# The next head's gates scaled on ScalarE, and two clamps placed at two levels of the recurrence

## The chip, the cores and the metric

The kernel runs on one core of one Trainium2 chip. The metric is the device time of one execution in microseconds (us). The core has a matrix engine (PE in the profile, with its weight loads as PEld), VectorE (DVE), ScalarE (ACT), GpSimd (POOL), a queue that issues nearly all transfers (SP, SPq in the profile) and 16 DMA engines. Each engine works through its own list of instructions in order and waits on semaphores that others raise.

## The reference, cut to what matters

The model is one encoder block over 1280 tokens of width 1024 (a prompt of 256 and a sample of 1024): layer norm, one wide projection, neighbourhood attention, a gated linear recurrence in two directions, a mix of the two branches, and an expert-choice feed-forward layer with 16 experts. The change lies in the recurrence, which has 4 heads of 128 channels:

```python
def forget_gates(z, lb):
    f = lb + (1.0 - lb) * jax.nn.sigmoid(z)
    log_f = jnp.log(jnp.maximum(f, F_MIN))
    k = (1.0 - lb) * jax.nn.sigmoid(-z)
    return k, log_f
# hgrn2_chunk_scan, for each direction: b = cumsum(log_f) within a chunk;
#   a[t, s] = sum_k q[t, k] * k[s, k] * exp(b[t, k] - b[s, k])   for s <= t
#   o = (q * exp(b)) @ S + a @ v;   S carries k and v from chunk to chunk
```

`lb` is one lower bound for each direction and channel. The gates of one head are two arrays of 128 channels by 1280 tokens, one for each direction `d`.

## The kernel before, in words

The stages follow one another, each in a block with a barrier behind it: front (layer norm and projection), attention, recurrence (`stage_recurrence`), mixing, choice of tokens, experts. The recurrence runs from about 612 to 1007 us of the span.

A head of the recurrence is computed in `R = 9` rounds, numbered `r` from 0. Rounds 0 and 1 make the keys for the carried state and round `r >= 2` makes the weights of one of `LEVELS = 7` levels, by which the 128x128 matrix of a chunk is filled in halves. A level takes these steps, one on each engine:

- POOL (L1027 `difference`) and DVE (L1297 `differences`) subtract running sums and write a slot of `W`; there are `WS = 3` slots, and a slot comes free when the matrix engine has read the level three before (`wait_slot`, L939).
- ACT (L1184 `exp`) takes the exponential of the whole slot, 128x2560.
- DVE (L1303 `weights`) multiplies by queries and keys: one product of 128x1280 at L1307 and two of 128x640 at L1314, then raises `w_ready`.
- PE (L1083 `pairs`) waits for that and runs 20 products of 128x128 (L1098).
- DVE (L1318 `gather`) copies what is valid of the level (L1331).

The product of round `r` is `pairs(r - 1)`. Between these products PE runs filler (L1047 `fill`): the last part of the wide projection, 40 units of two halves, 12 matmuls of 128x512 each half (L1062 to L1064). One half stands ahead of `pairs(n)` and one behind it. A unit needs a tile of the input (`fx`, two buffers, loaded at L977), its weights (`fw`, a ring of 11 blocks, loaded at L969 when a slab of 10 units ends) and one of two accumulators, which ACT empties at L1155 (`evict`).

During head `hd` the gates of head `hd + 1` are prepared. ACT calls `gates` in round 3, after its exponential: for each direction two sigmoids (L1165 into `f`, L1166 in place of the input `k`), then Silu of the queries (L1168). DVE calls `prepare` at the end of its own round 3 (L1371): for each direction it scales `k` (L1278), scales and shifts `f` (L1280), writes `lf = max(f, LN_SPLIT)` (L1283) and clamps `f` to the range from F_MIN to LN_SPLIT (L1285). ACT takes the logarithms of both in round 5 (L1170 `logarithms`, waiting for `clamped`), and DVE sums them with scans after its last round (L1288 `run_sums`). A function of another table costs ACT a load of a table (ACT_TABLE_LOAD).

The order of every engine's list is written out by hand in the four `head` functions. The lines that the change touches are L1160 to L1168 for ACT and L1271 to L1286, L1371 and L1378 for DVE.

Of the kernel before, what the change touches and what calls it, by code (L numbers as in the profile page):

```python
# [22 lines left out]
F32 = mybir.dt.float32  # L23
# [4 lines left out]
ACT = mybir.ActivationFunctionType  # L28
ALU = mybir.AluOpType
AX = mybir.AxisListType  # L30

P = 128
# [4 lines left out]
NT = T // P  # L37
# [3 lines left out]
HG_HEADS = 4  # L41
# [15 lines left out]
F_MIN = 1e-30  # L57
# [770 lines left out]
LN_SPLIT = 2.0 ** -60  # L828


def stage_recurrence(nc, ident, h, hT, xs, ws, lb_fwd, lb_bwd, o, room, carry, fw, fx, fw_in, fx_in,
# [24 lines left out]
    MASKS = 1 + 2 * LEVELS  # L856
    SETUP, PER = 5 + 3 + MASKS, 3 * 2
    U = len(LATER) * NT
    with ExitStack() as ctx:
        s = Stage(nc, ctx, "hg")  # L860
        k = [carry[:, 0:2 * T].rearrange("p (d t) -> p d t", d=2), s.sb("k", [P, 2, T])[:]]
        qT = [carry[:, 2 * T:3 * T], s.sb("qT", [P, T])[:]]
        v = [carry[:, 3 * T:4 * T].rearrange("p (c t) -> p c t", c=NT), s.sb("v", [P, NT, P])[:]]
        f, lf = s.sb("f", [P, 2, T]), s.sb("lf", [P, 2, T])
        E = s.sb("E", [P, 2, NT, P + 1])
        W = s.sb("W", [P, WS, 2, T])
        qi = room[:, 0:2 * T].rearrange("p (d t) -> p d t", d=2)
        kiT = room[:, 2 * T:4 * T].rearrange("p (d c t) -> p d c t", d=2, c=NT)
        decay = s.sb("decay", [P, 2, NT])
        S = s.sb("S", [P, 2, NT, P])  # L870
        A = room[:, 4 * T:5 * T]
        mask = s.sb("mask", [P, LEVELS, 4 * P], U8)
# [3 lines left out]
        lb, omlb = s.sb("lb", [P, 2, HG_HEADS]), s.sb("omlb", [P, 2, HG_HEADS])  # L876
# [9 lines left out]
             "lb_in", "iota_done", "q_done", "z_done", "clamped", "ln_done", "scanned",  # L886
             "dec_done", "pool_d", "dve_d", "exp_done", "w_ready", "qi_done", "ki_turned", "ki_copied", "l_mm",
             "a_done", "ds_mm", "s_made", "o_mm", "o_copied", "stored", "chain", "lb_ready"))
        fx_half = s.sem("fx_half")
        f_copied, f_stored = s.sem("f_copied"), s.sems("f_stored", 2)  # L890
        ki_groups = [(0, a, n) for a, n in CHUNK_GROUPS] + [(1, a, n) for a, n in reversed(CHUNK_GROUPS)]

# [57 lines left out]
        with nc.Block() as block:  # L950
# [193 lines left out]
            def _(act):  # L1144
# [15 lines left out]
                def gates(p, w):  # L1160
                    act.wait_ge(k_in[w], 32 * (p // 2) + 32)
                    if p >= 1:
                        act.wait_ge(scanned, 2 * p)
                    for d in range(2):
                        nc.scalar.activation(f[:, d], k[w][:, d], ACT.Sigmoid)  # L1165
                        nc.scalar.activation(k[w][:, d], k[w][:, d], ACT.Sigmoid, scale=-1.0).then_inc(z_done, 1)  # L1166
                    act.wait_ge(q_in[w], 16 * (p // 2) + 16)
                    nc.scalar.activation(qT[w], qT[w], ACT.Silu).then_inc(q_done, 1)  # L1168

# [64 lines left out]
            def _(dve):  # L1234
# [33 lines left out]
                          .then_inc(chain, 1)  # L1268
                        dve.wait_ge(chain, step.next())

                def prepare(p, w):  # L1271

                    count_of = Steps(PER)
                    count_of.base = SETUP + p * PER if p else SETUP - MASKS
                    for d in range(2):
                        dve.wait_ge(z_done, p * 2 + d + 1)
                        one_less, low = (x[:, d, p:p + 1] for x in (omlb, lb))
                        nc.vector.tensor_scalar(k[w][:, d], k[w][:, d], one_less, None, ALU.mult).then_inc(chain, 1)  # L1278
                        count_of.next()
                        nc.vector.tensor_scalar(f[:, d], f[:, d], one_less, low, ALU.mult, ALU.add).then_inc(chain, 1)  # L1280
                        dve.wait_ge(chain, count_of.next())

                        nc.vector.tensor_scalar(lf[:, d], f[:, d], LN_SPLIT, None, ALU.max).then_inc(chain, 1)  # L1283
                        dve.wait_ge(chain, count_of.next())
                        nc.vector.tensor_scalar(f[:, d], f[:, d], F_MIN, LN_SPLIT, ALU.max, ALU.min)\  # L1285
                          .then_inc(clamped, 1)  # L1286

                def run_sums(p):  # L1288
                    for d in range(2):
# [6 lines left out]
                def head(hd, w):  # L1296
                    def differences(r):  # L1297
                        if r >= 2:
                            wait_slot(dve, hd, r)
                            to, a, b = exponents(r)[3]  # L1300
                            nc.vector.tensor_tensor(to, a, b, ALU.subtract).then_inc(dve_d, 1)

                    def weights(r):  # L1303
                        dve.wait_ge(exp_done, hd * R + r + 1)
                        z, y = W[:, r % WS, 0], W[:, r % WS, 1]
                        if r >= 2:
                            nc.vector.tensor_tensor(z, z, qT[w], ALU.mult)  # L1307
                        else:
                            nc.vector.tensor_tensor(y, y, k[w][:, r], ALU.mult).then_inc(w_ready, 1)
                            return  # L1310
                        m = P >> (r - 1)
                        for side in range(2):
                            part = halves(chunked(y), m, side)
                            last = nc.vector.tensor_tensor(part, part, halves(chunked(k[w][:, side]), m, side),  # L1314
                                                           ALU.mult)
                        last.then_inc(w_ready, 1)

                    def gather(n):  # L1318

                        for g, (a, count) in enumerate(CHUNK_GROUPS):  # L1320
                            cols, width = slice(a * P, (a + count) * P), count * P
                            dve.wait_ge(l_mm, (hd * NL + n) * NG + g + 1)
                            if n == 0:
                                if hd >= 1:
                                    dve.wait_ge(stored, 16 * hd)
                                nc.vector.tensor_tensor(chunked(A[:, cols]), chunked(l_ps[g][:, 0:width]),
                                                        ident[:].unsqueeze(1).to_broadcast([P, count, P]), ALU.mult)\
                                  .then_inc(a_done, 1)
                            else:
                                dve.wait_ge(a_done, (hd * NL + n - 1) * NG + g + 1)  # L1330
                                nc.vector.copy_predicated(A[:, cols], mask[:, n - 1, 0:width], l_ps[g][:, 0:width])\  # L1331
                                  .then_inc(a_done, 1)

                    def states():

                        dve.wait_ge(dec_done, hd + 1)
                        steps = 0
                        for n, (d, a, count) in enumerate(ki_groups):
                            dve.wait_ge(ds_mm, hd * 2 * NG + n + 1)
                            order = list(range(a, a + count))  # L1340
                            for c in order if d == 0 else reversed(order):
                                to = c + 1 - 2 * d
                                if c in (ends, starts)[d]:
                                    continue
                                steps += 1
                                add = ring[n % NR][:, (c - a) * P:(c - a + 1) * P]
                                if c in (starts, ends)[d]:
                                    nc.vector.tensor_copy(S[:, d, to, :], add).then_inc(s_made, 1)
                                else:
                                    nc.vector.scalar_tensor_tensor(S[:, d, to, :], S[:, d, c, :], decay[:, d, c:c + 1],  # L1350
                                                                   add, ALU.mult, ALU.add).then_inc(s_made, 1)
                                dve.wait_ge(s_made, hd * NS + steps)

                    weights(0)
                    weights(1)
                    differences(2)
                    dve.wait_ge(q_done, hd + 1)
                    if hd >= 1:
                        dve.wait_ge(o_mm, hd * NG)
                    for d in range(2):  # L1360
                        nc.vector.tensor_tensor(qi[:, d], W[:, d, 0], qT[w], ALU.mult).then_inc(qi_done, 1)
                    gather(0)
                    for r in range(2, R):
                        if r + 1 < R:
                            differences(r + 1)
                        weights(r)
                        if r == 2:
                            states()
                        if r >= 3:
                            gather(r - 2)  # L1370
                        if r == 3 and hd + 1 < HG_HEADS:  # L1371
                            prepare(hd + 1, 1 - w)
                    if hd + 1 < HG_HEADS:
                        dve.wait_ge(pool_d, (hd + 1) * R)
                        run_sums(hd + 1)
                    gather(R - 2)

                prepare(0, 0)  # L1378
                masks()
                run_sums(0)  # L1380
                for hd in range(HG_HEADS):
# [650 lines left out]
PER = 2  # L2032
# [761 lines left out]
def build(nc, x, ln_in_g, ln_in_b, w_in, rpb, lb_fwd, lb_bwd, norm_g, w_na, w_hg, w_out, ln1_g, ln1_b, w_router,  # L2794
# [9 lines left out]
    with ExitStack() as ctx:  # L2804
        s = Stage(nc, ctx, "main")
        ident = s.sb("ident", [P, P])
        stage_consts(nc, ident)
        routing, mix = ctx.enter_context(ExitStack()), ctx.enter_context(ExitStack())
        with ExitStack() as bias:
            b = Stage(nc, bias, "bias")  # L2810
# [83 lines left out]
```

## Time and profile before

| what | value |
|---|---|
| median of 3 runs (2830.43 to 2831.44) | 2831.01 us |
| span of the profiled execution, first to last instruction | 2824.7 us |
| busy: PE, DVE, ACT, POOL | 2684.5 (95%), 1835.0 (65%), 1396.6 (49%), 557.2 (20%) us |
| mean granted PE clock | 0.977 of full speed |
| tile load of the filler (page, DMA issues) | 1024.0 KB, 5.3 us to landing |

No time of its own is listed for the profiled execution beside its span. The 6.3 us between span and median lie outside the first and the last instruction. A busy PE is not PE at its peak: the filler's matmuls are recorded as 0.39 to 0.40 us each and start 0.23 us apart, so busy time counts overlap once and says only that there is no hole.

### The profile page before, as it was taken

How to read it: one execution, taken by the hardware profiler on the slowest of the kernel's cores; microseconds unless marked ns; L12 is line 12 of the kernel's file. 1: busy time of each engine (PE TensorE's matmuls, PEld its weight loads, DVE VectorE, ACT ScalarE, POOL GpSimd, SP SyncE). 2: the span in 40 equal slices, each digit the busy share in tenths (PEclk: the TensorE clock that was granted, in tenths of full speed). 3: DMA queues.
4: the chain of work that ended last, by engine and by line, in shares of the span. 5: the costliest groups of instructions: out<-in, count | busy, mean ns of one | idle time of the engine just before them, and what ended most of it. 6: DMA issues, size and time to landing. Idle time of an engine off the chain costs nothing.

```text
span 2824.7 us, 44574 instructions
## 1 busy us (share of the span) xinstructions
PE 2684.5 (95%) x18224; PEld 2149.7 (76%) x18224; DVE 1835.0 (65%) x2309; ACT 1396.6 (49%) x1769; POOL 557.2 (20%) x492
## 2 busy tenths in 40 slices
PE   7999999988999979994999999999999999999998
PEld 5788887877887858883677777777777777777776
DVE  6212231768889756657577667677667667667888
ACT  2211221865555443341556656556656656656765
POOL 2000030004443523431001001101011001101334
PEclk9999999999999989996999999999999999999999
DMA  6478875766565554435678878878877878878984
GB/s 231 161 194 236 254 258 138 164 226 222 197 224 183 182 193 138 145 109 214 222 281 284 310 276 305 294 274 296 315 273 286 310 275 304 308 274 322 372 317 152
DMA packets 237452, 686.26 MB, mean 243 GB/s; under 512 B 18729, under 2 KB 65208, under 8 KB 232128
## 3 DMA queue, kind: packets, MB, share of 16 engines
q1 hardware_dynamic: 219904, 627.96, 62.5%
q0 software_dynamic: 17344, 55.44, 7.2%
q8 instruction: 145, 2.38, 0.3%
q14 instruction: 59, 0.48, 0.1%
HBM read 577.46 MB, written 105.88 MB: 242 GB/s over the span
## 4 chain that ended last, share of the span: by engine, by line
PE 49%; POOL 1%; DMA 1%; issue 1%; ACT 0%; DVE 0%; POOLq 0%; ACTq 0%; DVEq 0%
PE moe_strip L2453 12%; PE moe_up L2468 4%; PE moe_down L2468 4%; PE moe_gate L2468 4%; PE moe_gate L2470 4%; PE moe_down L2469 4%; PE moe_gate L2469 4%; PE moe_down L2470 4%; PE moe_up L2469 4%; PE moe_up L2470 4%; PE moe_up L2394 1%; POOL moe_minus_mean L2280 0%; PE moe_turn L2428 0%; DMA y<-moe_out_p,moe_at_out 0%; PE moe_gate L2403 0%
## 5 line engine op out<-in xcount | busy, mean ns | idle before, releaser
L2661 DVE TENSOR_TENSOR pieces_low<-pieces_raw,moe_high 128x1024 fp32r<-128x1024 f32 x768 | 893.2, 1217 | 355.2 <-PE moe_strip L2453 344.6
L2553 ACT ACTIVATE moe_high<-pieces_raw 128x1024 fp32r<-128x1024 f32 x768 | 769.3, 1051 | 360.2 <-PE moe_up L2470 195.8
L2453 PE MATMUL moe_strip<-pieces_raw,moe_xT_p 128*32 128x256 f32 x4096 | 230.5, 383 | 1.0 <-ACT moe_xT_p L2565 1.0
L2453 PEld LDWEIGHTS moe_strip<-pieces_raw,moe_xT_p 128*32 128x32 f32 x4096 | 130.6, 111 | 96.8 <-issue 13.9
L2468 PE MATMUL moe_gate<-moe_high,moe_xT 128*128 128x512 f32 x512 | 202.3, 395 | 2.0 <-DVE pieces_low L2661 1.9
L1031 POOL TENSOR_TENSOR hg_W<-hg_E 128x640 f32<-128x640 f32 (+1 forms) x92 | 164.4, 1814 | 196.8 <-PE hg_l L1098 99.5
L2468 PE MATMUL moe_up<-moe_high,moe_xT 128*128 128x512 f32 x512 | 202.9, 396 | 0.0
L2468 PE MATMUL moe_down<-moe_high,moe_hdn 128*128 128x512 f32 x512 | 202.6, 396 | 0.2 <-DVE pieces_low L2661 0.2
L2470 PE MATMUL moe_gate<-pieces_low,moe_xT 128*128 128x512 f32 x512 | 199.7, 390 | 0.0
L2469 PE MATMUL moe_up<-moe_high,moe_xT 128*128 128x512 f32 x512 | 199.6, 390 | 0.0
L2469 PE MATMUL moe_down<-moe_high,moe_hdn 128*128 128x512 f32 x512 | 199.5, 390 | 0.0
L2469 PE MATMUL moe_gate<-moe_high,moe_xT 128*128 128x512 f32 x512 | 199.5, 390 | 0.0
L2470 PE MATMUL moe_down<-pieces_low,moe_hdn 128*128 128x512 f32 x512 | 199.4, 390 | 0.0
L2470 PE MATMUL moe_up<-pieces_low,moe_xT 128*128 128x512 f32 x512 | 199.1, 389 | 0.0
L2244 POOL COPY moe_at_in<-main_picks 32x1 uint32<-32x1 uint32 (+1 forms) x32 | 10.4, 352 | 784.3 <-PE moe_up L2394 775.7
L492 DVE COPY fr_out<-fr_acc 128x512 f32<-128x512 f32 (+1 forms) x28 | 17.8, 634 | 194.1 <-PE fr_acc L361 106.7
L1062 PE MATMUL hg_facc<-bias_fw,bias_fx 128*128 128x512 f32 x320 | 132.2, 413 | 11.8 <-PEq L103 5.4
L1064 PE MATMUL hg_facc<-bias_fw,bias_fx 128*128 128x512 f32 x320 | 127.1, 397 | 0.0
L1063 PE MATMUL hg_facc<-bias_fw,bias_fx 128*128 128x512 f32 x320 | 126.9, 396 | 0.0
L2468 PEld LDWEIGHTS moe_up<-moe_high,moe_xT 128*128 128x128 f32 x512 | 96.0, 188 | 32.3 <-issue 13.2
L2468 PEld LDWEIGHTS moe_down<-moe_high,moe_hdn 128*128 128x128 f32 x512 | 96.1, 188 | 26.2 <-issue 6.6
L2453 PE MATMUL moe_strip<-pieces_raw,moe_hdn_p 128*32 128x256 f32 x2048 | 113.8, 380 | 0.0
(363 smaller groups left out, 5655.6 us busy)
## 6 DMA issues: line engine op xcount, KB each, us to landing
pieces_raw<-in_w_gate_e SPq DMA_DIRECT2D x128, 1024.0 KB, 5.3
pieces_raw<-in_w_up_e SPq DMA_DIRECT2D x128, 1024.0 KB, 7.0
pieces_raw<-in_w_down_e SPq DMA_DIRECT2D x128, 1024.0 KB, 5.1
bias_fx<-xs SPq DMA_DIRECT2D x40, 1024.0 KB, 5.3
fr_raw<-in_w_in SPq DMA_DIRECT2D x16, 1024.0 KB, 7.9
ws<-fr_late_split SPq DMA_DIRECT2D x32, 512.0 KB, 4.7
bias_fw<-ws SPq DMA_DIRECT2D x32, 512.0 KB, 8.6
mo_gates<-h SPq DMA_DIRECT2D x20, 512.0 KB, 4.5
```

What stands on the lines that cost most here:

```text
L492: nc.vector.tensor_copy(out[:, n, 0:width(i)], src).then_inc(copied[n], 1)
L1031: last = nc.gpsimd.tensor_tensor(to, a, b, ALU.subtract)
L1062: nc.tensor.matmul(f_acc[i % 2][:], fx[:, i % 2, 0, c, :], hi, start=(c == 0), stop=False)
L1063: nc.tensor.matmul(f_acc[i % 2][:], fx[:, i % 2, 0, c, :], lo, start=False, stop=False)
L1064: last = nc.tensor.matmul(f_acc[i % 2][:], fx[:, i % 2, 1, c, :], hi, start=False, stop=(c == KD - 1))
L2394: last = nc.tensor.transpose(to[:, k * P:(k + 1) * P], rows_s[:, (4 * j + k) * P:(4 * j + k + 1) * P], ident[:])
L2453: last = nc.tensor.matmul(strip_ps[j * CP:(j + 1) * CP, kind, :], x, raw[g % RAW][:, k * D + j * STRIP:k * D + (j + 1) * STRIP], start=sta ...
L2468: nc.tensor.matmul(to[:], x_k[:, kk, 0:CS], hi, start=(kk == 0), stop=False)
L2469: nc.tensor.matmul(to[:], x_k[:, kk, CS:2 * CS], hi, start=False, stop=False)
L2470: return nc.tensor.matmul(to[:], x_k[:, kk, 0:CS], lo, start=False, stop=(kk == count - 1))
L2553: nc.scalar.activation(high[:, g % HI, cols], raw[g % RAW][:, cols], ACT.Copy).then_inc(hi_done, 1)
L2661: nc.vector.tensor_tensor(low[g % RAW][:, cols], raw[g % RAW][:, cols], high[:, g % HI, cols].bitcast(F32), ALU.subtract).then_inc(lo_done, 1)
```

## The change

ACT takes over the scaling of `k` and of `f` for heads 1 to 3, behind the four sigmoids of round 3 and ahead of Silu. DVE keeps the two clamps of each direction; direction 0 is clamped in round 3 and direction 1 in round 4. Head 0's gates, which are made before the first round, stay as they were (`prepare_first`). `decay` is allocated ahead of `W` instead of behind it, and an unused tensor of 32 bytes per partition is allocated on the right side of the memory for the whole program.

```diff
-        E = s.sb("E", [P, 2, NT, P + 1])
+        E, decay = s.sb("E", [P, 2, NT, P + 1]), s.sb("decay", [P, 2, NT])
         W = s.sb("W", [P, WS, 2, T])
...
-        decay = s.sb("decay", [P, 2, NT])
...
-        fx_half = s.sem("fx_half")
+        fx_half, z_opened = s.sem("fx_half"), s.sem("z_opened")
...
                     for d in range(2):
                         nc.scalar.activation(f[:, d], k[w][:, d], ACT.Sigmoid)
-                        nc.scalar.activation(k[w][:, d], k[w][:, d], ACT.Sigmoid, scale=-1.0).then_inc(z_done, 1)
+                        nc.scalar.activation(k[w][:, d], k[w][:, d], ACT.Sigmoid, scale=-1.0)\
+                          .then_inc(z_opened if p else z_done, 1)
+                    for d in range(2 if p else 0):
+                        one_less, least = (x[:, d, p:p + 1] for x in (omlb, lb))
+                        act.wait_ge(z_opened, (p - 1) * 2 + d + 1)
+                        nc.scalar.activation(f[:, d], f[:, d], ACT.Identity, bias=least, scale=one_less)
+                        nc.scalar.activation(k[w][:, d], k[w][:, d], ACT.Copy, scale=one_less).then_inc(z_done, 1)
...
-                def prepare(p, w):
+                def clamp(d, count):
+
+                    nc.vector.tensor_scalar(lf[:, d], f[:, d], LN_SPLIT, None, ALU.max).then_inc(chain, 1)
+                    dve.wait_ge(chain, count)
+                    nc.vector.tensor_scalar(f[:, d], f[:, d], F_MIN, LN_SPLIT, ALU.max, ALU.min).then_inc(clamped, 1)
+
+                def prepare_first():
...
+                def prepare(p, d):
+
+                    dve.wait_ge(z_done, p * 2 + d + 1)
+                    clamp(d, SETUP + PER + (p - 1) * 2 + d + 1)
...
-                        if r == 3 and hd + 1 < HG_HEADS:
-                            prepare(hd + 1, 1 - w)
+                        if r in (3, 4) and hd + 1 < HG_HEADS:
+                            prepare(hd + 1, r - 3)
...
-                prepare(0, 0)
+                prepare_first()
...
+        ctx.enter_context(nc.sbuf_tensor("side_pad", [P, 8], F32, side="right"))
```

`prepare_first` holds the eight instructions of the old `prepare` for head 0, the last two of each direction through `clamp`.

## Rows read from the trace of the kernel before

**Rows 1.** Windows: heads 0 and 3. Start:end, length, each engine's busy time (instructions), clock, DMA.
```profile
663.00:743.20 80.20, 75.32 (x446) 66.27 (x444) 68.28 (x96) 42.71 (x39) 32.92 (x20) 0.98 0.58 200
...
926.60:1000.60 74.00, 73.74 (x447) 65.17 (x446) 54.12 (x70) 23.62 (x22) 32.03 (x19) 1.00 0.52 173
```

**Rows 2.** Timeline of PE: start, duration, engine, line, operation, tiles, [idle before <- releaser].
```profile
685.05 2.39 PE L1098 MATMUL hg_l<-hg_W 128*128 128x128 f32 x20
687.20 0.48 PE L1062 MATMUL hg_facc<-bias_fw,bias_fx 128*128 128x512 f32 x1
...
692.78 2.39 PE L1098 MATMUL hg_l<-hg_W 128*128 128x128 f32 x20
...
705.36 3.93 PE L1098 MATMUL hg_l<-hg_W 128*128 128x128 f32 x20 [4.70 <-DVE bias_table L1331]
...
714.61 2.39 PE L1098 MATMUL hg_l<-hg_W 128*128 128x128 f32 x20
...
793.17 4.07 PE L1098 MATMUL hg_l<-hg_W 128*128 128x128 f32 x20 [4.70 <-DVE bias_table L1331]
```

**Rows 3.** Windows: the products behind the hole of head 0, columns as in rows 1.
```profile
705.30:709.20 3.90, 3.84 (x21) 3.87 (x22) 3.90 (x6) 3.89 (x5) 0.00 (x0) 0.60 1.01 422
```

**Rows 4.** Waits of PE's weight loads: total us, times, longest.
```profile
PEld hg_l L1098 <- DVE hg_W L1314: 15.3, 3, 5.1
```

**Rows 5.** Timeline of DVE in rounds 3 and 4 of head 0.
```profile
689.13 1.74 DVE L1278 TENSOR_SCALAR hg_k<-hg_k,hg_omlb 128x1280 f32<-128x1280 f32 x1
690.79 1.99 DVE L1280 TENSOR_SCALAR hg_f<-hg_f,hg_omlb,hg_lb 128x1280 f32<-128x1280 f32 x1
...
694.42 0.88 DVE L1278 TENSOR_SCALAR hg_k<-hg_k,hg_omlb 128x1280 f32<-128x1280 f32 x1
695.22 0.94 DVE L1280 TENSOR_SCALAR hg_f<-hg_f,hg_omlb,hg_lb 128x1280 f32<-128x1280 f32 x1
...
699.75 1.96 DVE L1301 TENSOR_TENSOR hg_W<-hg_E 128x640 f32<-128x640 f32 x1
...
703.03 1.55 DVE L1314 TENSOR_TENSOR hg_W<-hg_W,wroom 128x640 f32<-128x640 f32 x2
```

**Rows 6.** Source line L1283, all instances: shortest, median, longest ns.
```profile
L1283 DVE TENSOR_SCALAR hg_lf<-hg_f x8: 827/828/1806, 629.0 to 873.8; 128x1280 f32<-128x1280 f32 x8
```

**Rows 7.** Windows: two rounds of head 3, which prepares no gates, columns as in rows 1.
```profile
953.20:968.66 15.46, 15.46 (x90) 13.48 (x89) 11.54 (x14) 5.66 (x4) 9.59 (x6) 1.00 0.52 170
```

**Rows 8.** Timeline of DVE in head 1: a pair of products that ran beside POOL's.
```profile
805.77 3.67 DVE L1314 TENSOR_TENSOR hg_W<-hg_W,hg_k 128x640 f32<-128x640 f32 x2
```

**Rows 9.** Timeline of ACT: around the gates in head 0, and one eviction in head 1.
```profile
677.51 1.26 ACT L1166 ACTIVATE hg_k<-hg_k 128x1280 f32<-128x1280 f32 x1
...
681.25 0.58 ACT L1155 ACTIVATE bias_table<-hg_facc 128x512 f32<-128x512 f32 x1
685.25 0.60 ACT L1155 ACTIVATE hg_fout<-hg_facc 128x512 f32<-128x512 f32 x1 [3.41 <-PE hg_facc L1064]
...
687.16 2.35 ACT L1195 ACTIVATE hg_W<-hg_W 128x2560 f32<-128x2560 f32 x1
...
785.79 0.60 ACT L1155 ACTIVATE hg_fout<-hg_facc 128x512 f32<-128x512 f32 x1 [3.46 <-PE hg_facc L1064]
```

**Rows 10.** Groups by line and shape, ACT: count | busy us, mean ns | idle before.
```profile
L807 ACT ACTIVATE na_sc<-na_sc,na_nmax 128x512 f32<-128x512 f32 x32 | 23.0, 719 | 2.3 <-DVE na_nmax L765 1.5
...
L389 ACT ACTIVATE fr_late_split<-fr_late 128x512 fp32r<-128x512 f32 x32 | 20.2, 630 | 110.7 <-DMA fr_late<-in_w_in 110.5
```

**Rows 11.** Timeline of SP: the first loads of the filler's next weights in head 0.
```profile
697.97 3.04 SPq L969 DMA_DIRECT2D bias_fw<-ws  x5
```

**Rows 12.** Source line L969, all 21 loads: us from issue to landing.
```profile
DMA to landing us min/median/max: 3.2/6.2/10.2
```

**Rows 13.** Source line L1307, by tile: shortest, median, longest ns.
```profile
L1307 DVE TENSOR_TENSOR hg_W<-hg_W,wroom x14: 1476/1484/2573, 669.8 to 903.4; 128x1280 f32<-128x1280 f32 x14
L1307 DVE TENSOR_TENSOR hg_W<-hg_W,hg_qT x14: 1472/1492/2576, 757.8 to 988.2; 128x1280 f32<-128x1280 f32 x14
```

More of the change, by code:

```diff
@@ L1269, in masks @@
                         dve.wait_ge(chain, step.next())
-                def prepare(p, w):
+                def clamp(d, count):
[3 more added lines that the diff above has]
+                def prepare_first():
                     count_of = Steps(PER)
-                    count_of.base = SETUP + p * PER if p else SETUP - MASKS
+                    count_of.base = SETUP - MASKS
                     for d in range(2):
-                        dve.wait_ge(z_done, p * 2 + d + 1)
-                        one_less, low = (x[:, d, p:p + 1] for x in (omlb, lb))
-                        nc.vector.tensor_scalar(k[w][:, d], k[w][:, d], one_less, None, ALU.mult).then_inc(chain, 1)
+                        dve.wait_ge(z_done, d + 1)
+                        one_less, low = (x[:, d, 0:1] for x in (omlb, lb))
+                        nc.vector.tensor_scalar(k[0][:, d], k[0][:, d], one_less, None, ALU.mult).then_inc(chain, 1)
                         count_of.next()
@@ L1281, in prepare @@
                         dve.wait_ge(chain, count_of.next())
[L1283 to L1286, printed above, removed]
+                        clamp(d, count_of.next())
+                def prepare(p, d):
+                    dve.wait_ge(z_done, p * 2 + d + 1)
+                    clamp(d, SETUP + PER + (p - 1) * 2 + d + 1)
                 def run_sums(p):
```

## The prediction

> **What bounds the kernel now.** I read the page first. PE is busy 95% of the span, so in most stages the other engines don't matter; only a hole in PE is worth anything. The table of windows, taken head by head, finds where the holes are: head 0 of the recurrence takes 80.20 us from its first product to its last level, head 3 takes 74.00 us, and both run the same 447 or so matmuls. In head 3 PE has no hole to speak of (73.74 us busy) at a clock of 1.00; in head 0 it is busy 75.32 us at 0.98 [rows 1]. Head 3 is the only one that prepares no gates.
>
> The timeline of PE shows the difference at one place. Level products normally start 7.73 us apart (685.05, 692.78), with two halves of filler between them. The next one, `pairs(3)`, was due 7.73 us after 692.78, at 700.51; it starts at 705.36 behind a hole of 4.70 us and then takes 3.93 us instead of 2.39 [rows 2]. In that stretch the granted clock is 0.60, that is, most of it at 1.2 GHz instead of 2.4, after PE had stood idle [rows 3]. The hole has the same 4.70 us in head 1 [rows 2] and there are three of them in all, one in each head that prepares [rows 4].
>
> Who releases it: the timeline names a gather (L1331), but that engine's gather had long been done; the list of waits names L1314, the second half of `weights(4)` [rows 4], which ends at 703.03 + 1.55 = 704.58 [rows 5]. DVE comes late to it because `prepare` runs without a break from 689.13 to 699.75, 10.6 us [rows 5].
>
> **What the change removes.** Four of the eight instructions of `prepare` leave DVE: 1.74 + 1.99 + 0.88 + 0.94 = 5.55 us in head 0 [rows 5], likewise in heads 1 and 2. One direction's two clamps, 0.83 us each or 1.80 beside POOL [rows 6], move behind `weights(4)`; in head 0 both of those were of the slow kind, 3.6 us. `weights(4)` can so be ready up to 5.55 + 3.6 = 9.2 us earlier, and 704.58 - 700.51 = 4.1 us are needed. That closes the hole and, with it, the slow stretch behind it. The worth per head, measured over both: from `pairs(2)` at 692.78 to `pairs(4)` at 714.61 are 21.83 us [rows 2], and at 7.73 a level they would be 15.46, so 6.37 us. Three heads: 19.1 us. Head 0's excess over head 3 in the windows, 6.2 us, says the same [rows 1].
>
> **What is late next: DVE in round 4.** `pairs(4)` is then due at 700.51 + 7.73 = 708.24. Two rounds of head 3 keep DVE busy 11.54 us of 15.46, which leaves 3.9 us idle [rows 7]. To this comes the lead that DVE has on PE. In head 0 the gather of `pairs(1)` ends at 689.13, so from there to 708.24 are 19.1 us, and the work in them is the two clamps (3.3 to 7.2 us, rows 6), two rounds' work less one gather (11.54 less about 1.7, so 9.8) and the first third of that gather (0.6): 13.7 to 17.6 us. It fits, by 1.5 us or more. Against it: work of DVE that meets POOL's subtractions is slowed, a pair of L1314 from 1.55 to 3.67 us [rows 5, 8], and the shifted order lets `weights(4)` or `weights(5)` begin just when POOL has been released by a level product. One such pair more makes 15.8 to 19.7 us. So I expect from nothing to 2 us of new wait at `pairs(4)`, likelier in head 1, where the exponential of round 5 also can't start before the eviction of 785.79 [rows 9]. I take 0.5 us a head, 1.5 in all, the bounds being 0 and 6.
>
> **What ScalarE pays.** Four activations of 128x1280 more in each of three heads. Nearest row: the sigmoid of the same shape, 1.26 us, of which the next hides 0.1 [rows 9]. The trace has no scaling by a column of this shape; an exponential with a column as bias takes 719 ns at 128x512, a plain one 630 [rows 10], so 0.09 us for each column, one for Copy and two for Identity. Then 4 x 1.16 + 6 x 0.09 = 5.2 us a head, with 4.6 and 5.4 as ends. The new waits on `z_opened` name sigmoids issued two and more instructions earlier and cost about nothing; behind them on ACT stand Silu, the evictions and the exponential of round 4.
> What hides it in head 0: after the first eviction ACT was idle 3.41 us [rows 9]. The eviction of 681.25 moves to 686.4; its accumulator is wanted by the filler at 687.20 [rows 2], so it is in time by 0.2 us, or late by up to 0.2. The second eviction goes from 685.25 to 687.0, and the exponential from 687.16 to about 688.9, which ends at 691.3. DVE has `weights(4)` in its list after a clamp and a difference, at 689.13 + 3.6 + 0.8 = 693.5 at the latest and 691.6 at the earliest, so the exponential is not the later one. In head 1 the parity of the units is the other one and ACT waits longer for PE after its gates, so nothing moves. I put ScalarE's part on the path at 0, with 0 to 0.5 us a head as bounds.
> SP has a small share in this: its queue holds the store of a unit ahead of the next tile's load, so a later eviction delays that load in heads 0 and 2 by under 2 us; the tile takes 5.3 us (the table above) and is wanted 7.7 us later. Nothing.
>
> A rule of the Trainium skill speaks against the move: "ScalarE: Activation LUTs", section "Rules for kernel authors", gives multiplications and minima to VectorE and not to ScalarE, since VectorE is faster per element. The rows agree on speed (0.88 against 1.26 us). By that rule alone the edit would cost about 4 x 1.3 less 5.55, near zero, and gain nothing; it does not ask which engine is late, and here only DVE is. The same page, section "What ACT_TABLE_LOAD costs", has each column operand at about 93 ns; the trace agrees with 89. Its section "Table sets: the hidden batching unit" has copy and identity in every set, by which no table load is added; no run here shows that yet.
>
> **The filler's weights, in head 0 alone.** The hole of head 0 also covered a transfer. The first five blocks of the next slab are issued from 697.97 to 701.0 [rows 11]. Unit 10 used to start at 709.05, now at 702.7. It reads one of these blocks from about 704.8 on and four from 705.6 to 707.7. At 3.2 us for the first and the median of 6.2 for the last [rows 12] they land from 701.2 to 707.2, in time by about 0.5 us. At the longest landing of 10.2 us it would be 3.5 us late, once. I take 0, and 3.5 as the bound.
>
> **The new places in memory.** `W` moves by a few ten bytes and all tensors of the right side by 32. The same product reads its queries from a tensor of the right side in 1484 ns and from one of the left side in 1492 [rows 13], so a place changes at most 0.5%, of engines that are not the bound. Zero; plus or minus 1 us.
>
> **Sum.** 19.1 - 1.5 = 17.6 us less. The profiled span would be 2824.7 - 17.6 = 2807.1, and with 6.3 us outside of it, as now, 2813.4 against the median of 2831.0 (0.6%). What can be told from no change with this kernel is about 0.2%, 5.7 us.
>
> **Rivals.**
> 1. *The hole moves to `pairs(4)`.* DVE meets POOL at each of its steps, is 2 us or more late in each head, and PE's clock falls again in part. For it: slow instructions are common in these rounds [rows 5, 8]. Against it: 1.5 us of slack by the count above. It keeps 2 to 3.5 us a head, so the gain is 9 to 13 us: 2818 to 2822. Chance 0.17.
> 2. *Nothing is gained since the path was not DVE's list.* If `weights(4)` waited for something else just behind (its exponential, or the slot of POOL), removing DVE work would only turn busy time into waiting. Against it: DVE is busy without a break from 689.13 on, and the exponential of round 4 ended at 689.5 [rows 5, 9], 12 us before it was used. A weaker form is the late weights of the filler. 2826 to 2831. Chance 0.07.
> 3. *Slower: ScalarE becomes late.* The place is the eviction of 681.25 in heads 0 and 2, which decides when the filler may take its accumulator at 687.20. From 5.4 us of added ScalarE work on, every further microsecond is idle PE; table loads in front of Identity and behind it, or scaling at twice the sigmoid's price (10 us a head), would make 4 to 5 us of hole with the clock's 1.5 behind it, and the clamps of round 3, waiting on `z_done`, would push `weights(4)` as well: 6 us for the eviction and up to 6 again at `pairs(3)`, against 6.4 saved. It ends at 2835 to 2845. Against it: the rows for column operands. Chance 0.04.
>
> **Chances.** The forecast 0.72, the rivals 0.17, 0.07 and 0.04. The likeliest one's own range is 2811 to 2817; reaching into rival 1 the range for 8 in 10 is 2811 to 2822. Faster by over 0.2%: 0.72 + 0.17 and a little of rival 2, 0.90; within 0.2%: 0.06; slower: 0.04.
>
> **What the profile after would show.** Right: no wait of 4.7 us at L1098 in heads 0 to 2; these products at 2.39 us; windows of heads 0 to 2 shorter by about 6 us each, head 3 unchanged at 74; DVE's busy time less by about 17 us and ScalarE's more by about 15; the same number of table loads. Rival 1 would show waits at the product 7.7 us later, released by L1314 again. Rival 3 would show L1062 waiting for ACT at L1155. A wait of L1062 for `bias_fw` in head 0 would be the transfer. The prediction is wrong if the holes go and the time does not, which would mean that a later stage gives the time back.

## The result, and the profile after

The changed kernel takes 2808.2 us (median of 4 runs, 2806.69 to 2811.0) against 2831.16 us, ratio 0.9927, 95% interval 0.9915 to 0.9939. (A ratio here is an estimate from the single runs with its interval. It is not the quotient of the two medians, which is 0.9919 and lies inside the interval.) The forecast was 2813.4 us in a range from 2811 to 2822: the direction held, and so did the mechanism in the recurrence, but the time lies 2.8 us below the range. Timed twice more beside the kernel before (e1 and e12 below) it gave 2810.47 against 2829.61 (0.9933, 0.9920 to 0.9946) and 2809.18 against 2827.98 (0.9931, 0.9917 to 0.9945), so 19 us rather than 23. The forecast fall of 17.6 us (0.9938) lies in each of these intervals. One execution of the kernel before beside e12, 3078.42 us at a granted clock of 0.839, is a slow one and is in no ratio.

The windows of the heads come first, of the kernel before (heads 1 and 2, which stand beside rows 1) and then of the changed kernel (heads 0 to 3). Columns are those of rows 1.

```profile
749.00:832.90 83.90, 75.99 (x446) 66.36 (x445) 74.11 (x98) 42.31 (x39) 35.88 (x21) 0.98 0.62 216
838.80:920.80 82.00, 75.72 (x447) 66.35 (x445) 73.95 (x98) 42.74 (x39) 35.22 (x21) 0.98 0.59 199
```

```profile
659.50:733.50 74.00, 73.79 (x446) 64.97 (x444) 65.86 (x92) 48.10 (x43) 33.40 (x20) 1.00 0.63 217
739.40:819.10 79.70, 74.14 (x447) 64.84 (x445) 72.22 (x94) 48.07 (x44) 36.98 (x21) 1.00 0.66 228
824.90:900.90 76.00, 73.83 (x446) 65.17 (x446) 70.72 (x94) 48.56 (x43) 36.00 (x21) 1.00 0.64 215
906.80:981.40 74.60, 73.56 (x447) 65.14 (x446) 54.54 (x70) 23.62 (x22) 30.94 (x19) 1.00 0.52 171
```

The first fence is the kernel before, the second the changed one. Heads 0, 1 and 2 are shorter by 6.2, 4.2 and 6.0 us, head 3 is 0.6 longer. Head 0 now takes what head 3 took [rows 1], at a clock of 1.00. The timeline of PE has the cause, line by line against [rows 2] (L1098 of before is L1097 now):

```profile
681.64 2.39 PE L1097 MATMUL hg_l<-hg_W 128*128 128x128 f32 x20
...
689.35 2.39 PE L1097 MATMUL hg_l<-hg_W 128*128 128x128 f32 x20
...
697.06 2.39 PE L1097 MATMUL hg_l<-hg_W 128*128 128x128 f32 x20
...
704.77 2.39 PE L1097 MATMUL hg_l<-hg_W 128*128 128x128 f32 x20
...
788.64 2.47 PE L1097 MATMUL hg_l<-hg_W 128*128 128x128 f32 x20 [2.00 <-DVE bias_table L1343]
```

`pairs(3)` follows `pairs(2)` after 7.71 us and takes 2.39 us, where it took 3.93 behind a hole of 4.70. One hole is new: 2.00 us ahead of `pairs(4)` in head 1 (788.64). The list of waits again names VectorE's second products as the real releaser (L1326 now):

```profile
PEld hg_l L1097 <- DVE hg_W L1326: 2.4, 1, 2.4
```

VectorE's list in head 1 shows what made it late. First it stood idle for 0.99 us ahead of `weights(4)`, waiting for ScalarE's exponential of round 4; in heads 0 and 2 it did not wait there. Then two stretches of L1326 took 3.76 and 3.67 us instead of 1.55, and L1319 took 2.56 instead of 1.49. The second fence has the exponential, and the third POOL's subtractions, which ran beside the slow stretches.

```profile
772.71 1.49 DVE L1319 TENSOR_TENSOR hg_W<-hg_W,hg_qT 128x1280 f32<-128x1280 f32 x1 [0.99 <-ACT hg_W L1200]
774.12 3.76 DVE L1326 TENSOR_TENSOR hg_W<-hg_W,hg_k 128x640 f32<-128x640 f32 x2
777.80 1.68 DVE L1343 COPY_PREDICATED bias_table<-hg_mask,hg_l 128x512 f32<-128x512 uint8 x3
779.37 0.82 DVE L1278 TENSOR_SCALAR hg_lf<-hg_f 128x1280 f32<-128x1280 f32 x1
780.23 0.83 DVE L1280 TENSOR_SCALAR hg_f<-hg_f 128x1280 f32<-128x1280 f32 x1
780.97 0.82 DVE L1313 TENSOR_TENSOR hg_W<-hg_E 128x640 f32<-128x640 f32 x1
781.70 2.56 DVE L1319 TENSOR_TENSOR hg_W<-hg_W,hg_qT 128x1280 f32<-128x1280 f32 x1
784.18 3.67 DVE L1326 TENSOR_TENSOR hg_W<-hg_W,hg_k 128x640 f32<-128x640 f32 x2
```

```profile
770.33 2.34 ACT L1200 ACTIVATE hg_W<-hg_W 128x2560 f32<-128x2560 f32 x1
```

```profile
773.49 5.60 POOL L1030 TENSOR_TENSOR hg_W<-hg_E 128x640 f32<-128x640 f32 x3 [3.19 <-PE hg_l L1097]
781.30 5.87 POOL L1030 TENSOR_TENSOR hg_W<-hg_E 128x640 f32<-128x640 f32 x3 [2.22 <-PE hg_l L1097]
```

The exponential itself is no later than it was: it starts 7.09 us behind `pairs(1)` of head 1, 7.12 before. VectorE, with less in its list, now gets there first.

The busy times of the whole span, against the table of the kernel before:

```profile
PE 2675.0 (95%) x18224; PEld 2143.6 (76%) x18224; DVE 1828.3 (65%) x2297; ACT 1411.5 (50%) x1781; POOL 561.3 (20%) x492
```

ScalarE's rose by 14.9 us, as forecast (about 15). VectorE's fell by 6.7 us only, where about 17 were forecast. The scaling did leave it (20.3 us before, 3.7 now), but its second products (L1314, now L1326) took 69.5 us in the recurrence instead of 54.3: much of what left came back as slower work.

ScalarE's part: the scalings with two columns and with one, and what became of the evictions and of the exponential of round 4 in head 0, against [rows 9].

```profile
L1170 ACT ACTIVATE hg_f<-hg_f,hg_lb,hg_omlb x6: 1438/1442/1445, 675.3 to 844.8; 128x1280 f32<-128x1280 f32 x6
...
L1171 ACT ACTIVATE hg_k<-hg_k,hg_omlb x4: 1348/1352/1355, 676.6 to 846.1; 128x1280 f32<-128x1280 f32 x4
```

```profile
683.05 0.58 ACT L1154 ACTIVATE bias_table<-hg_facc 128x512 f32<-128x512 f32 x1
683.53 0.59 ACT L1154 ACTIVATE hg_fout<-hg_facc 128x512 f32<-128x512 f32 x1
...
685.43 2.35 ACT L1200 ACTIVATE hg_W<-hg_W 128x2560 f32<-128x2560 f32 x1
```

Against the plain 1.26 us that is 0.09 us for each column operand, as forecast. The first eviction ends at 683.63; the filler, at its own pace behind `pairs(1)`, wants the accumulator 2.1 us after 681.64, at 683.8, and gets it. In the traces ScalarE loads a table 19 times in the recurrence before and 19 times after, so Identity and Copy added none.

Where the 18.2 us between the two profiled spans went: PE starts the filler at 614.82 instead of 617.68, 2.9 us earlier, before anything of the gates; from there to the first product of the mixing stage (1019.80 before, 1000.18 now) 16.8 us; and 1.4 us are lost again behind it, up to the end.

```profile
614.82 0.76 PE L1061 MATMUL hg_facc<-bias_fw,bias_fx 128*128 128x512 f32 x1 [5.38 <-PEq L103]
...
1000.18 0.80 PE L1625 MATMUL mo_acc<-mo_wb_hi,mo_act_hi 128*128 128x512 f32 x1 [12.84 <-DVE mo_act_lo L1862]
```

The first of these was in no step of the forecast, and the new places in memory are the only part of the change that reaches the front stage.

### The profile page after: what moved, and what is told of

The parts are those of the page before. It is cut to its first block, busy times and chain, and to the rows that moved or that the text cites. A ratio compares the mean times of both kernels' runs of the same rounds, so it can differ in the third digit from the quotient of the medians.

```text
span 2806.5 us, 44574 instructions
## 1 busy us (share of the span) xinstructions
PE 2675.0 (95%) x18224; PEld 2143.6 (76%) x18224; DVE 1828.3 (65%) x2297; ACT 1411.5 (50%) x1781; POOL 561.3 (20%) x492
## 4 chain that ended last, share of the span: by engine, by line
PE 49%; DMA 1%; POOL 1%; DVE 1%; issue 1%; ACT 0%; POOLq 0%; DVEq 0%; ACTq 0%
PE moe_strip L2465 11%; PE moe_down L2480 4%; PE moe_down L2481 4%; PE moe_down L2482 4%; PE moe_up L2480 4%; PE moe_gate L2480 4%; PE moe_gate L2482 4%; PE moe_gate L2481 4%; PE moe_up L2481 4%; PE moe_up L2482 4%; PE moe_up L2406 1%; PE moe_turn L2440 0%; POOL moe_minus_mean L2292 0%; DMA out<-moe_norm_x 0%; DMA y<-moe_out_p,moe_at_out 0%
## 5 line engine op out<-in xcount | busy, mean ns | idle before, releaser
L411 ACT ACTIVATE fr_out<-fr_acc 128x512 f32<-128x512 f32 (+1 forms) x38 | 21.4, 563 | 184.4 <-PE fr_acc L366 114.2
```

Of the source, the lines that this page charges most:

```text
L411: nc.scalar.activation(out[:, n, 0:width(i)], src, ACT.Copy).then_inc(copied[n], 1)
```

## The experiments

Times are medians; a ratio is against the kernel before on the same chip, with its 95% interval. e1 to e4 and e9 to e11 ran on one chip, e5 to e7 on a second, e12 to e15 on a third.

**The change again, and its two halves in memory.** For e1 nothing is edited. e2 takes the new places back, e3 has them alone:

```diff
# e2, against the changed kernel
-        E, decay = s.sb("E", [P, 2, NT, P + 1]), s.sb("decay", [P, 2, NT])
+        E = s.sb("E", [P, 2, NT, P + 1])
+        decay = s.sb("decay", [P, 2, NT])   # behind W and kiT again
-        ctx.enter_context(nc.sbuf_tensor("side_pad", [P, 8], F32, side="right"))
# e3, against the kernel before: the opposite
```

> The changed kernel once more, beside the kernel before on one chip, because the time fell by 23 us where the two profiled spans differ by 18. Theory A (the recurrence gives all of it, and the profiled execution of the kernel before was a quick one): 16 to 18 us less than the kernel before on the same chip. Theory B (the new places in memory make the matrix engine a little quicker in the front stage too, where the profiled span lost 3 us): 20 to 23 us less again.

> The changed kernel with decay allocated behind W again and without the 32 bytes on the right side; all instructions as in the changed kernel. Theory A: as the changed kernel within 1 us. Theory B: 3 to 6 us more than the changed kernel, and the front stage 3 us longer in the trace.

> The kernel before with the new places alone (decay ahead of W, 32 bytes on the right side). Theory A: the time of the kernel before within 1 us. Theory B: 3 to 6 us less than the kernel before.

Measured: e1 2810.47 us (0.9933, 0.9920 to 0.9946); e2 2812.81 (0.9941, 0.9929 to 0.9954); e3 2825.17 (0.9986, 0.9977 to 0.9995), the kernel before 2829.61. e3 alone is 4.4 us faster, clear of no change; e1 and e2 differ by 2.3 us, which their intervals don't part. e1 lies between the two theories (19.1 us less, against 16 to 18 and 20 to 23). Theory B holds in its sign and in the traces, where the size is plainer than in the times: e2's attention stage ends at 610.5 us, e1's at 607.9. e2 is also the change without its new places, 16.8 us below the kernel before. Three single edits of the kernel before, one execution each, take the places apart:

```diff
# e9: 32 bytes on the right side       e11: 64 bytes
+        ctx.enter_context(nc.sbuf_tensor("side_pad", [P, 8], F32, side="right"))    # e11: [P, 16]
# e10: decay ahead of W
```

> The kernel before with the 32 bytes on the right side and nothing else. Theory P (the matrix engine streams an operand a little faster or slower according to its place; carry on the right side is the moving operand of the front stage): the front stage ends 2.5 us earlier, as with both moves, and the levels of the recurrence keep 7.73 us. Rival (W's place does it, or chance from run to run): the front stage ends at 610.5 to 611.2 us as in the kernel before.

> The kernel before with decay ahead of W and nothing else, so that W lies 80 or 96 bytes further. Theory P: the front stage as in the kernel before, and the levels of the recurrence come 7.705 us apart and not 7.727, since L1098 reads both its operands from W. Rival: no difference anywhere.

> The kernel before with 64 bytes on the right side. If the place counts by its remainder to 64 bytes, the front stage ends as in the kernel before (610.5 to 611.2); if by any distance, it ends near 608.

Measured, beside 2828.92 us for one execution of the kernel before: e9 2825.63, e10 2828.82, e11 2828.52. Single executions of the kernel before differ by more than that (2826.06 to 2834.11 on this chip), so the traces decide. The timelines of PE: the end of the attention stage, then `pairs(1)` and `pairs(2)` of head 0; e9, e10 and e11 in this order.

```profile
607.81 1.09 PE L739 MATMUL na_o<-na_pT,na_v 128*64 128x128 f32 x16 [0.48 <-DVE na_out L786]
...
681.38 2.39 PE L1098 MATMUL hg_l<-hg_W 128*128 128x128 f32 x20
...
689.11 2.39 PE L1098 MATMUL hg_l<-hg_W 128*128 128x128 f32 x20
```

```profile
610.68 1.09 PE L739 MATMUL na_o<-na_pT,na_v 128*64 128x128 f32 x16 [0.49 <-DVE na_out L786]
...
683.13 2.39 PE L1097 MATMUL hg_l<-hg_W 128*128 128x128 f32 x20
...
690.84 2.39 PE L1097 MATMUL hg_l<-hg_W 128*128 128x128 f32 x20
```

```profile
610.77 1.09 PE L739 MATMUL na_o<-na_pT,na_v 128*64 128x128 f32 x16 [0.48 <-DVE na_out L786]
...
683.08 2.39 PE L1098 MATMUL hg_l<-hg_W 128*128 128x128 f32 x20
...
690.80 2.39 PE L1098 MATMUL hg_l<-hg_W 128*128 128x128 f32 x20
```

With 32 bytes the stages ahead of the recurrence end at 607.8, without or with 64 at 610.7; the level distance stays 7.73. With `decay` ahead of `W` the stages ahead are as before and the level distance is 7.71. All eleven traces with the 32 bytes end that stage at 606.7 to 608.8, all five with none or 64 (the kernel before, e2, e4, e10, e11) at 610.5 to 611.2, so chance is out. Theory P holds in what it says of the two stages. It named the wrong operand, though. `carry` is the only tensor of the right side that the front stage reads, and PE reads it in two ways: as the operand that it streams (L359 to L361) and as the weights that it loads (L364 to L366, where it streams `front_xT`). The time is in the second. The groups of the front stage, of the kernel before and then of the changed one:

```profile
L366 PE MATMUL fr_acc<-carry,front_xT_lo 128*128 128x512 f32 x160 | 65.1, 407 | 0.0
L365 PE MATMUL fr_acc<-carry,front_xT_hi 128*128 128x512 f32 x160 | 64.4, 403 | 0.0
```

```profile
L366 PE MATMUL fr_acc<-carry,front_xT_lo 128*128 128x512 f32 x160 | 64.0, 400 | 0.0
L365 PE MATMUL fr_acc<-carry,front_xT_hi 128*128 128x512 f32 x160 | 63.7, 398 | 0.0
```

From start to start, three such matmuls take 0.702 us before and 0.690 in the changed kernel (means of some 110 triples in each trace); 0.690 in e9, 0.701 in e11, 0.702 in e10. Where `carry` is streamed the three take 0.703 and 0.700, and 0.700 in e11 too. Those that read `fr_w_hi` and `fr_w_lo`, which did not move, kept 0.68. 160 triples of the first kind and 128 of the second make some 2.4 of the 2.9 us by which the front stage's last product comes earlier (481.77 before, 478.88 now). Why a place decides is open. The return with 64 bytes fits a rule by the remainder to 64, but only two distances on one side and one on the other were tried.

**Splitting without taking anything off VectorE.** e4 is the kernel before with `prepare` of one direction in each of rounds 3 and 4:

```diff
-                        if r == 3 and hd + 1 < HG_HEADS:
-                            prepare(hd + 1, 1 - w)
+                        if r in (3, 4) and hd + 1 < HG_HEADS:
+                            prepare(hd + 1, 1 - w, (r - 3,))
```

> The kernel before with prepare of direction 0 in round 3 and of direction 1 in round 4, all four instructions of each still on VectorE, nothing on ScalarE. If the hole at pairs(3) is VectorE being late by its list alone, it goes here too: prepare of direction 0 takes 3.4 to 6 us, so weights(4) is ready at about 698 to 699 in head 0 against 700.5 due. The rest comes later: direction 1 adds 3.4 to 6 us more ahead of pairs(4), which then waits 2 to 5 us in each head. In all 4 to 12 us less than the kernel before. The rival (the amount of work taken from VectorE counts, not its place): 0 to 3 us less.

Measured: 2829.05 us, ratio 1.000 (0.9991 to 1.0009). My 4 to 12 us were wrong and the rival's 0 to 3 right: the hole went from `pairs(3)` to `pairs(4)` with all that belongs to it.

```profile
700.02 2.47 PE L1098 MATMUL hg_l<-hg_W 128*128 128x128 f32 x20 [0.45 <-DVE bias_table L1331]
...
711.61 4.61 PE L1098 MATMUL hg_l<-hg_W 128*128 128x128 f32 x20 [3.64 <-DVE bias_table L1331]
```

0.45 + 3.64 us of wait and 2.2 us of slow products behind it make 6.3 us; the one hole before made 4.70 + 1.54 = 6.2. So the gain of the change comes from the 5.55 us a head of work taken from VectorE; moving half of the list by a level is worth nothing by itself.

**Other places for the clamps.** e5 and e13 do both directions in round 3; e6 and e14 do the second in round 5 and the logarithms in round 6; e12 is the changed kernel beside e13 and e14; e15 leaves the clamps of heads 1 to 3 out but for 8 of 1280 columns, and takes both logarithms from `f` without the factor. (e8, the same with the factor left in, gave no time.)

```diff
# e5 and e13, against the changed kernel
-                        if r in (3, 4) and hd + 1 < HG_HEADS:
-                            prepare(hd + 1, r - 3)
+                        if r == 3 and hd + 1 < HG_HEADS:
+                            prepare(hd + 1, 0)
+                            prepare(hd + 1, 1)
# e6 and e14, against the changed kernel
-                        if r == 5 and hd + 1 < HG_HEADS:
+                        if r == 6 and hd + 1 < HG_HEADS:
                             logarithms(hd + 1)
...
-                        if r in (3, 4) and hd + 1 < HG_HEADS:
-                            prepare(hd + 1, r - 3)
+                        if r in (3, 5) and hd + 1 < HG_HEADS:
+                            prepare(hd + 1, (r - 3) // 2)
# e15, against the changed kernel: both tensor_scalar of prepare on lf[:, d, 0:8] and f[:, d, 0:8]
```

> The changed kernel with both directions' clamps in round 3 and none in round 4. In head 1 of the changed kernel VectorE reaches pairs(4) 2.0 us late. Theory: the late work is only moved: round 3 holds four clamps (5.3 to 7.2 us beside GpSimd) and weights(4) becomes ready about 1 us early to 1.5 us late for pairs(3), whose hole is 0 to 1.5 us, while the 2.0 us at pairs(4) go. Time within 2 us of the changed kernel. Rival (what counts is that the clamps sit at two levels): a hole of 3 us or more at pairs(3) in each head and 6 us more.

> The changed kernel with direction 1's clamps in round 5 and both directions' logarithms in round 6 on ScalarE. Theory: pairs(4) of head 1 loses its hole of 2.0 us and the slow products behind it (up to 1.7 us), nothing is late in turn, since round 5 has 3.9 us of idle VectorE in two rounds to give: 2 to 4 us less than the changed kernel. Rival: the hole goes to pairs(5) and the time stays.

> The changed kernel beside the two other places of the clamps, all on one chip, because they were timed on different chips. 18 to 21 us less than the kernel before.

> Both directions' clamps in round 3 again. If splitting them over two levels is worth something, this is 2 us or more above the changed kernel; the traces so far (0.4 us of hole at three places against 2.0 us and up to 1.4 us of slow clock at one) say 1 to 3 us below it.

> Direction 1's clamps in round 5 and the logarithms in round 6 again. The traces say 2 to 4 us below the changed kernel and 1 to 2 below the version with all clamps in round 3; the intervals may not part them.

> The changed kernel with the clamps of heads 1 to 3 done on 8 columns only and the second logarithm taken without its factor: it leaves that arithmetic out and shows what VectorE's part of the gates still costs. Theory: only the hole at pairs(4) of head 1 is left to remove, 2 to 4 us less than the changed kernel. Rival (VectorE's load still slows the levels elsewhere, through its meetings with GpSimd): more than 6 us less.

| kernel | us | before | ratio, interval |
|---|---|---|---|
| e5, both in round 3 | 2806.71 | 2827.83 | 0.9918 (0.9903 to 0.9934) |
| e6, second in round 5 | 2805.35 | 2827.83 | 0.9914 (0.9900 to 0.9927) |
| e12, the change | 2809.18 | 2827.98 | 0.9931 (0.9917 to 0.9945) |
| e13, both in round 3 | 2806.49 | 2827.98 | 0.9923 (0.9909 to 0.9937) |
| e14, second in round 5 | 2806.86 | 2827.98 | 0.9924 (0.9910 to 0.9938) |
| e15, hardly any clamps | 2807.49 | 2827.98 | 0.9925 (0.9909 to 0.9941) |

On one chip the two other places are 2.3 to 2.7 us below the change, as expected of both (that e14 would be 1 to 2 us below e13 did not come), and level with e15; the intervals don't part them from the change. So clamps at two neighbouring levels show no gain over clamps at one. The traces say why all are near: e13's `pairs(3)` waits 0.37, 0.36 and 0.37 us in heads 0 to 2, and e14's only wait at a level product is 0.55 us, at `pairs(5)` of head 1, where e12's `pairs(4)` of head 1 waits 1.99 us and then takes 3.92. Even with hardly any clamps head 1 keeps such a wait, one level on:

```profile
788.21 3.92 PE L1097 MATMUL hg_l<-hg_W 128*128 128x128 f32 x20 [1.99 <-DVE bias_table L1343]
```

```profile
796.69 2.47 PE L1097 MATMUL hg_l<-hg_W 128*128 128x128 f32 x20 [1.66 <-DVE bias_table L1346]
```

The first fence is e12, the second e15. In e15 L1329 (the old L1314) took 3.7 us three times in a row ahead of it, and ahead of the last of them VectorE had stood idle 1.44 us for ScalarE's exponential of round 6:

```profile
789.93 2.38 DVE L1322 TENSOR_TENSOR hg_W<-hg_W,hg_qT 128x1280 f32<-128x1280 f32 x1 [1.44 <-ACT hg_W L1200]
792.24 3.67 DVE L1329 TENSOR_TENSOR hg_W<-hg_W,hg_k 128x640 f32<-128x640 f32 x2
```

So a wait of this kind in head 1 does not need the clamps. What is left beside them are the meetings of VectorE and POOL and the time at which ScalarE's exponential comes; no experiment takes either away, and their shares stay open. My 2 to 4 us for e15 came to 1.7, within its noise.

**Twice the scaling on ScalarE.**

```diff
# e7, in gates, behind the two scalings of each direction, which raise z_scaled
+                        act.wait_ge(z_scaled, (p - 1) * 4 + 2 * d + 2)
+                        nc.scalar.activation(f[:, d], f[:, d], ACT.Copy)
+                        nc.scalar.activation(k[w][:, d], k[w][:, d], ACT.Copy).then_inc(z_done, 1)
```

> The changed kernel with each scaling on ScalarE followed by a plain copy of the same tile in place, in heads 1 to 3: 4 more activations a head, about 4.9 us. It tests how much cover ScalarE's list has. By the forecast's count the eviction at 683 us of head 0 then ends 5 us after the filler wants its accumulator: a wait of L1061 for ScalarE of 4 to 5 us in heads 0 and 2, none in head 1, a granted clock that falls behind it, so 8 to 13 us more than the changed kernel. Rival (ScalarE has room): 0 to 2 us.

Measured: 2826.72 us against 2827.83 (0.9996, 0.9987 to 1.0006), some 17 us more than the changed kernel (by the ratios, 0.9996 against 0.9931 to 0.9933), where 8 to 13 were expected: the whole gain is gone. Waits of the filler for ScalarE's eviction in heads 0, 1 and 2 (duration of the one matmul, then the wait):

```profile
687.33 0.77 PE L1061 MATMUL hg_facc<-bias_fw,bias_fx 128*128 128x512 f32 x1 [4.66 <-ACT bias_table L1154]
...
777.93 0.47 PE L1061 MATMUL hg_facc<-bias_fw,bias_fx 128*128 128x512 f32 x1 [2.84 <-ACT hg_fout L1154]
...
866.67 0.47 PE L1061 MATMUL hg_facc<-bias_fw,bias_fx 128*128 128x512 f32 x1 [4.42 <-ACT hg_fout L1154]
```

The place and the 4 to 5 us were as expected in heads 0 and 2. I had expected none in head 1; there ScalarE stood idle 2.27 us in the changed kernel, less than the 5 that were added. Behind the wait of head 0 the granted clock is 0.50 for the next 4.1 us, that is, 1.2 GHz. In head 0 the change has spent ScalarE's cover to the last 0.2 us (683.63 against 683.8).

## Why the prediction was right and wrong

- *The hole at `pairs(3)`, its releaser L1314 and its worth.* Right, and shown: 3 x 6.37 = 19.1 us less a rest; the heads gave 6.2, 4.2 and 6.0, 16.4 in all. e4 shows that it is the work taken away that closes it, and e2, which has no new places, fell by 16.8 us (13.0 to 20.1) where the sum had 17.6.
- *The new hole at `pairs(4)`.* Forecast 0 to 2 us in a head, likelier in head 1, 1.5 in all; measured 2.00 us in head 1 and none in heads 0 and 2. Right in size and place. The count allowed for slow pairs, but not for the 0.99 us in which VectorE waits for the exponential of round 4. The hole is in head 1 alone in e1, e2 and e12 too; the products behind it took 2.47 us in the first trace, 3.62 in e1, 3.92 in e12.
- *VectorE's busy time.* Forecast less by about 17 us, measured 6.7. The scaling left, but more of the products met POOL. It cost little, since only what comes late for a level counts.
- *ScalarE.* 5.2 us a head forecast from 0.09 for a column. From 675.26, the start of the first scaling, to 680.58, where Silu's table load begins, are 5.3 us in head 0. The eviction was in time; e7 shows that 5 us more are not.
- *The filler's weights in head 0.* Forecast in time by 0.5 us, with 3.5 us late as the bound. The first trace has no such wait, but the filler waited for `bias_fw` in head 0 for 0.56 us in e12, 0.47 in e2, 0.92 in e13 and 1.18 in e14, and in head 2, which the forecast left out, for up to 1.64 (e5). Zero was a little too kind; the bound held.
- *The new places.* This is the step that failed in kind: "a place changes at most 0.5%, of engines that are not the bound. Zero; plus or minus 1 us." I compared two tensors as read by VectorE. What moved is `carry`, which PE reads in every second slab of the front stage, and PE is the bound there: three matmuls with their weights from it went from 0.702 to 0.690 us. The front stage's last product comes 2.9 us earlier in the first pair of traces, and e3 is 4.4 us (1.4 to 6.5) below the kernel before.
- *The base.* The other mis-sized term. I put 6.3 us outside of the span, and so does the text above the prediction. In every run of either kernel whose span is listed, time and span differ by 1.7 to 1.9 us (2808.32 against 2806.5). So the profiled execution of the kernel before took about 2826.5 us and was quicker than the median shown. The forecast span of 2807.1 us was nearly met (2806.5); with 1.8 us outside it the sum would have said 2808.9. The kernel before ran from 2822.25 to 2834.11 us over all comparisons. A forecast of 17.6 us taken from 2831.0 has this scatter in it: the fall from 2831.16 to 2808.2 is 23.0, in the two other comparisons 19.1 and 18.8. A range whose lower end lay only 2.4 us below the forecast left no room for it; the lower end should have been near 2806.

That the forecast span came out so close is in part luck: the 2.9 us of the front stage were not in it, the heads gave 1.2 us less than 17.6, and 1.4 us were lost behind the recurrence.

What stays open is how much of the first comparison's 23 us is scatter between executions; the two profiled spans hold 18.2 of them.

## What to carry to other kernels

Where one engine waits for another at one place of a pipeline, count the work in the late engine's list up to the next two deadlines: in e4 half of the work was moved past the first deadline and the hole moved with it, and taking work off the list removed it. Before work goes to an idle engine, find the idle stretch that stands directly behind it, not the engine's share: ScalarE was 49% busy and had room for 5 us a head, not for 10. Work taken off an engine that shares its time with another can come back as slower work: 16.6 us left VectorE and its busy time fell by 6.7. A change that shifts allocations is a change to every stage that reads them; look at what the matrix engine reads, as weights too, and test with the allocation alone.

## What the runs showed of the hardware

- The spacing of back-to-back 128x512 matmuls depends on the place of an operand, and most on that of the weights: 0.702 us for three that load their weights from `carry` where it was, 0.690 with it moved by 32 bytes, 0.701 with 64. Where `carry` is streamed it is 0.703 and 0.700, and 0.700 with 64 bytes too. `W`, from which a level product reads both operands, moved by the 80 bytes of `decay` gave 7.71 instead of 7.73 us a level.
- Two products of 128x640 on VectorE take 1.55 us alone, 2.66 when POOL's subtractions begin just behind their start, and 3.67 to 3.76 when these are already running; a clamp of 128x1280 takes 0.83 or 1.6 to 1.9. The Trainium skill, "SBUF — State Buffer", section "SBUF: two separate sides", has a port pair that VectorE and GpSimd take in turns for a whole instruction, also for a VectorE operation with two inputs in this memory against a GpSimd operation that reads it. The trace agrees: both the products and POOL's subtractions are of this kind, and the product of 128x1280 took 2.56 us beside them and 1.49 alone.
- A column operand on ScalarE costs 0.09 us at 1280 elements; Identity and Copy brought no table load (19 before and after).
